# Where the later rows stand beside the first half's layers, and which engine makes a row's gate and diagonals

## The reference, cut to what matters

```
expert, gate = top 16 of 256 candidate pairs, for each of 8 heads      # 128 experts for a token
h   = gelu(einsum('thkd,td->thk', expert_u[expert], x))
out = einsum('thk,thkd->td', gate * h, expert_v[expert])
```

```
s = q k^T * scale, causal;  p = softmax(s);  a = p0 - lam * p1   (layer 1),   a = p   (layer 2)
h = h + (a v) @ w_o
h = h + square(relu(rms_norm(h) @ w_up)) @ w_down
```

## Time and profile before

| | us |
|---|---|
| median of 3 runs | 3049.65 (3047.44 to 3058.9) |
| the profiled execution | 3047.7, its span 3045.9 |
| half 0 from its first product to the end of its second MLP | 1302 to 2315 |
| half 1 | 2327 to 3046 |

### The profile page before, as it was taken

How to read it: one execution, slowest core, us unless ns; L and a number is a source line. 1 busy time by engine, 2 the same in 40 slices (tenths; PEclk the granted TensorE clock), 3 DMA queues, 4 the chain that set the end, 5 groups by cost and what they waited for, 6 DMA issues and landing times. The chain is left out here.

```text
span 3045.9 us, 49365 instructions
## 1 busy us (share of the span) xinstructions
PE 2585.2 (85%) x18974; PEld 1960.1 (64%) x18974; DVE 1763.8 (58%) x3863; ACT 1388.3 (46%) x3129; POOL 1648.2 (54%) x973
## 2 busy tenths in 40 slices
PE   6997977987877777687698997679997999999998
PEld 3865965743333232265477776458776979989998
DVE  5686433767777776765654457565446463256323
ACT  2231222243344343456865456765554454444543
POOL 3822113834444443466287776358883618852785
PEclk8988978999999999888799998889997999999999
DMA  7210013289999999779789997989995415542453
GB/s 293 101 59 26 4 57 152 93 331 421 421 421 421 421 421 415 316 300 401 284 325 401 377 389 296 376 314 393 402 409 218 152 34 175 187 134 74 157 186 115
DMA packets 140538, 797.61 MB, mean 262 GB/s; under 512 B 15504, under 2 KB 18704, under 8 KB 67600
## 3 DMA queue, kind: packets, MB, share of 16 engines
q0 software_dynamic: 73728, 536.90, 43.4%
q1 hardware_dynamic: 65856, 253.09, 23.3%
q10 hardware_dynamic: 720, 4.46, 0.3%
HBM read 787.84 MB, written 6.55 MB: 261 GB/s over the span
## 5 line engine op out<-in xcount | busy, mean ns | idle before, releaser
L303 POOL TENSOR_TENSOR wls<-raws,whs 128x1024 fp32r<-128x1024 f32 (+1 forms) x256 | 612.0, 2400 | 370.3 <-ACT whs L297 368.3
L1998 PE MATMUL ps<-ts,whs 128*128 128x256 f32 x1424 | 292.2, 306 | 27.5 <-DVE ts L2093 19.6
L1754 POOL DMA_INDIRECT raw<-in_peer_uv,un x205 | 209.3, 1021 | 191.7 <-PE ps L1778 87.6
L297 ACT CAST whs<-raws 128x1024 fp32r<-128x1024 f32 (+1 forms) x256 | 263.9, 1036 | 96.8 <-PE ps L2576 35.2
L303 POOL TENSOR_TENSOR wlw<-raws,whw 128x1024 fp32r<-128x1024 f32 x112 | 267.8, 2404 | 70.4 <-ACT whw L297 69.7
L1847 ACT ACTIVATE un<-un 128x1 f32<-128x1 f32 x384 | 77.6, 202 | 445.6 <-DVE scratch L1892 432.0
L1998 PEld LDWEIGHTS ps<-ts,whs 128*128 128x128 f32 x1424 | 239.6, 205 | 56.1 <-issue 26.8
L1892 DVE SCALAR_TENSOR_TENSOR scratch<-raw,ps 128x1024 f32<-128x1024 f32 x149 | 181.4, 1217 | 133.4 <-DMA raw<-in_peer_uv,un 120.2
L2576 PE MATMUL ps<-ts,whs 128*128 128x256 f32 x1216 | 228.7, 289 | 0.2 <-DVE ts L2629 0.2
L1998 PE MATMUL ps<-ts,wls 128*128 128x256 f32 x712 | 209.8, 295 | 0.0
L303 POOL TENSOR_TENSOR wl<-raw,wh 128x2048 fp32r<-128x2048 f32 x23 | 107.1, 4660 | 186.0 <-ACT wh L297 186.0
(11 more groups left out here) (443 smaller groups left out, 6883.2 us busy)
## 6 DMA issues: line engine op xcount, KB each, us to landing
raws<-in_w_up SPq DMA_DIRECT2D x128, 512.0 KB, 4.2
raws<-in_w_down SPq DMA_DIRECT2D x128, 512.0 KB, 4.7
scratch<-in_ada_w SPq DMA_DIRECT2D x17, 1024.0 KB, 13.2
raws<-in_w_qk SPq DMA_DIRECT2D x32, 512.0 KB, 8.5
raw<-in_w_in SPq DMA_DIRECT2D x11, 1024.0 KB, 5.3
raw<-in_peer_w_q SPq DMA_DIRECT2D x8, 1024.0 KB, 8.0
raws<-in_w_v SPq DMA_DIRECT2D x16, 512.0 KB, 5.7
raws<-in_w_o_a SPq DMA_DIRECT2D x16, 512.0 KB, 4.0
```

Of the source, the lines that this page charges most:

```text
L297: e.copy(self.wh[h][:, 0:width], self.raw[slot][:, 0:width]).then_inc(*self.tick("hi", key))
L303: e.tensor_tensor(self.wl[h][:, 0:width], self.raw[slot][:, 0:width], self.wh[h][:, 0:width].bitcast(F32), ALU.subtract).then_inc(*self.ti ...
L1754: e.indirect_dma_start(self.rows[r], None, self.d["peer_uv"], index).then_inc(*self.tick(f"row{r}", n, 16))
L1998: ins = e.matmul(o[:, 0:256], l, r, start=k == 0 and i == 0, stop=k == nk - 1 and i == 2)
```

## The change

- `RATE` falls from 1.1 to 1.0.
- The turns of `attention` weigh 0.01 when n is even and 3.6 when n is odd, instead of 1.2 each.
- For the stacked rows ScalarE only applies Gelu. VectorE multiplies `each32` (32 columns of constants) by Gelu's result and by the gate in one `tensor_scalar` with two column operands (`dve_diagonal`). It stands in VectorE's queue in step n behind the dot of row n+1, and TensorE waits for it in step n+1. The first 256 rows are as before.

The counters give, for half 0 (rows by stage, the same on every engine):

| stage | before | after |
|---|---|---|
| join, q, k, v of layer 1 | 29 | 27 |
| attention of layer 1 | 25 | 32 |
| the norm behind it, w_o | 11 | 10 |
| MLP 1 | 71 | 64 |
| projections of layer 2 | 17 | 16 |
| attention of layer 2 | 25 | 32 |
| w_o of layer 2 | 9 | 8 |
| MLP 2 | 70 | 64 |
| final norm of half 0 | 0 | 4 |

```diff
-RATE = 1.1
+RATE = 1.0
...
-                e.wait_ge(*self.at(A_, ("diag", n)))
+                e.wait_ge(*self.at(D_ if self.stacked(n) else A_, ("diag", n)))
...
         e.wait_ge(*self.at("peer_dve", ("dot", n)))
+        if self.stacked(n):
+            e.activation(gelus[:, c], dots[:, c], ACT.Gelu, bias=0.0, scale=1.0).then_inc(*self.tick(S, ("gelu", n)))
+            return
...
-        if self.stacked(n):
-            e.activation(diag[:, 0:32], self.each32, ACT.Identity, bias=0.0,
-                         scale=weight[:, c]).then_inc(*self.tick(S, ("diag", n)))
...
             if n + 1 < 512:
                 self.dve_dot(e, n + 1)
+            if 0 <= n < 512 and self.stacked(n):
+                self.dve_diagonal(e, n)
...
+    def dve_diagonal(self, e, n):
+
+        k = n % 128
+        e.wait_ge(*self.at("peer_act", ("gelu", n)))
+        e.wait_ge(*self.at("peer_pe", ("acc", n - 4)))
+        e.tensor_scalar(self.diag[1][n % 4][:, 0:32], self.each32, self.gelus[1][:, k:k + 1], self.gate[n // 128][:, k:k + 1],
+                        ALU.mult, ALU.mult).then_inc(*self.tick("peer_dve", ("diag", n)))
...
-            yield 1.2
+            yield 3.6 if n % 2 else 0.01
```

More of the change, by code:

```diff
@@ L1853, in act_weight @@
         e.wait_ge(*self.at(S, ("weight", n)))
-        diag = self.diag[n >= 128][n % 4]
-        if self.stacked(n):
-            e.activation(diag[:, 0:32], self.each32, ACT.Identity, bias=0.0,
-                         scale=weight[:, c]).then_inc(*self.tick(S, ("diag", n)))
-        else:
-            e.activation(diag, self.C("ident"), ACT.Identity, bias=0.0,
-                         scale=weight[:, c]).then_inc(*self.tick(S, ("diag", n)))
+        e.activation(self.diag[n >= 128][n % 4], self.C("ident"), ACT.Identity, bias=0.0,
+                     scale=weight[:, c]).then_inc(*self.tick(S, ("diag", n)))
     def act_join(self, e, tt):
```

## The result

The changed kernel takes 3082.3 us (median of six runs, 3075.7 to 3090.5), the kernel before 3051.3 (six runs, 3044.9 to 3058.9). The ratio is 1.0107, with a 95% interval of 1.0087 to 1.0126: slower by 31 us. The forecast was 3033 in a range of 3008 to 3058, so it had the wrong sign and the time lies outside the range.

A forecast was written before the change was run, and what follows sets the result against it. DMA was taken to bound the MLPs, ScalarE's table loads the first attention's middle. MLPs -33, attentions 0, late diagonals +10, other stages +3, end +5 gave -15, with a more even period -17: 3033 us, range 3008 to 3058.

The forecast's parts named there:

- The MLPs, -33: Both MLPs: transfers set their time, so 64 rows each instead of 71 and 70 save 33 us together.
- The price of a held diagonal: VectorE's diagonal in the MLPs: 0.15 us itself, plus a mean 0.64 us a row waiting for GpSimd's subtractions.
- Rival D: Diagonals make VectorE the MLPs' bound, each waiting 2.1 us: +38, 3088 us, chance 0.13.
- TensorE one row of lag and late diagonals: MLPs: TensorE falls back 2.9 us once and follows late diagonals by up to 2.1 us: +10 together (0 to +20).
- Attentions, 0: Both attentions: seven more rows each cost nothing; between -4 each at the high clock and +7 each at the low.
- the forecast's five terms: Attention's pair of turns: Gelu and table load 1.57, exponentials 0.81, scores 2.13 or 1.30, maximum to dot 2.13, dots 4.50 us.
- Other stages, +3: Projections, w_o stages and norms: fewer rows -3, diagonals on VectorE's path +6, together +3 (-5 to +15).
- The end of half 0, +5: Behind the second MLP and final norm: four rows' steps now come there and delay the join, +5 (0 to +8).

The follow-up runs named there:

- the half gathers: Kernel before, with the gathers of the 256 later rows bringing 1024 of 2048 columns, half the bytes: 3001.9 us, ratio 0.9829.
- the half matmuls: Kernel before, with four of each later row's eight matmuls left out, except the first and last row of every 32: 3050.9 us, ratio 0.9989.
- the odd form: Changed kernel, its diagonal tensor_scalar writing 33 columns and reading its table as 3 times 11 with a gap: 3036.4 us; on the old schedule 3048.5 us.
- The idle operation: Kernel before, diagonals on ScalarE, with VectorE also making gate times diagonal behind each dot into columns nobody reads: 3081.6 us, ratio 1.0097.
- the schedule alone: Kernel before with only the change's rate 1.0 and turn weights 3.6 or 0.01, gate and diagonal staying on ScalarE: 3042.1 us, ratio 0.9973.

## Why the prediction was wrong

- **The MLPs, -33.** The mechanism (transfers set the MLPs) is confirmed by the half gathers and the half matmuls. The size depends on what stands beside it. Moving the rows gave -15 with ScalarE's diagonals, grouped, -23 with the same rows spread evenly, and -29 from the odd form on the old schedule (265.3 and 262.2) to the odd form on the new one (245.9 and 253.0). In the changed kernel it was +7, as held diagonals ate it: 269.0 and 274.6, 45 us more for the pair than in the odd form.
- **The price of a held diagonal is the step that failed.** I took 0.15 us plus a mean wait of 0.64, together 0.79; the means are 0.85 and 0.88 in the two MLPs. The sum is near, by some luck: the 0.15 I took for a quarter of the columns is never under 0.288. What was wrong is what I did with it. I gave 5 us per MLP for the path, with 2.1 us as the longest delay, and laid the rest beside VectorE's slack. But most of the holding comes in holds of 5 us, one diagonal in ten, because GpSimd's subtractions stand two and two without a gap; the earlier trace rows had three in a row in 7.40 us, and I read it as 2.4 us each. All six of the first MLP are on the path, 30 us, and against the odd form the MLPs are 23 and 22 us longer where I had 5 each.
- **Rival D had the right engine and almost the right time (3088) by a sum that did not occur.** It wanted every diagonal to be late by 2.1 us. Its sign, "the dots no longer wait for the DMA", came true: 2.8 us in place of 92.
- **"TensorE one row of lag and late diagonals", +10,** looked for the cost at TensorE. The idle operation, which TensorE doesn't wait for, costs 30 us as well, so VectorE's own lateness is enough for a loss of this size. It was run with the old schedule only, where it falls on other stages; that the changed kernel's MLPs pay for VectorE's lateness and not for TensorE's waits (20 us in each) is argued from it, not shown.
- **Attentions, 0.** The second is at 0 (96.1 for 96.1), the first at +19.5. A pair of turns was to last 10.3 to 11.1 us. From one load of Gelu's table to the next it was 11.67 us with four rows and 10.35 with three in the second attention; in the first it was 13.68 and 11.46, and 16.6 in the first two pairs. In the pair from 1477.00 to 1490.68 three of the forecast's five terms came true at the low clock (0.63 granted there): 0.81, 2.13 and 2.13. The two others failed. The dots took 5.27 for 4.50, four in the place of 3.57 and 1.35 us apart for 1.26, as a diagonal stands between them. And from the last dot's end to the exponential it was 3.34 us for 1.57, because the chain had left out a wait: ScalarE's exponential table is loaded only when the maximum of the even turn's scores (L2492) is there, and TensorE makes these scores (L2318) behind a row's accumulation, which had waited for its diagonal.

```profile
1481.19 1.08 PE L1778 MATMUL ps<-un 128*32 128x256 f32 x8 [0.34 <-DVE un L1884]
...
1482.20 0.80 PE L2318 MATMUL ps<-k,q 64*128 64x128 f32 x4
...
1484.32 1.28 ACT L2399 ACT_TABLE_LOAD   x1 [1.81 <-DVE kept L2492]
```

  This wait stands ahead of seven table loads of the first attention, 12.4 us in all; with the schedule alone it is 2.9, in the kernel before none. The schedule alone makes +13 in the first attention, and the same rows spread evenly +10, so the larger part is the rows' number. Why the kernels divide 211 to 220 us so differently between the two attentions stays open, and so do the two pairs of 16.6.
- **Other stages, +3,** was +14 (layer 1's projections and w_o, layer 2's projections and w_o), and the holds cover it: with the odd form these stages are 16 us shorter than in the changed kernel. **The end of half 0, +5,** measured +3.
- **The size of the schedule's own gain** was overrated in the sum: -33 in the MLPs was not set against what the rows cost in the attentions. Its real balance is -7 to -8 us with ScalarE's diagonals, -12 with free ones and 0 with held ones.

## What to carry to other kernels

Before small work is moved to VectorE, look at what GpSimd runs beside it and for how long without a gap. Here the longest such stretch was a better guide to the price than its share of the time, and what stands behind on VectorE pays it. An operand in PSUM, or a shape that can't be read in two halves, kept a VectorE operation free of it here, for 10 ns at most. Where the time of a stage is set by buffers that go round (gather, dot, diagonal, accumulation), a step made later by one turn lengthens the trip (246 to 281 us and 253 to 288 here). And the even spread with the diagonals left on ScalarE (3034.9 us) was as good as the best kernel with the right values.

## What the runs showed of the hardware

- VectorE's 0.3 us operation on SBUF alone was held for up to 5.15 us beside two GpSimd subtractions of 2.4 us, and was not let in between them. All six long ones of the first MLP start within GpSimd's gather instruction, 0.3 to 0.5 us ahead of the first subtraction's record (1640.94 and 1641.38), so the hold may begin with the gather; the sixteen others of the two MLPs that started within a gather took 0.3 us, and this was not settled.
- The dots show the same, in the kernel before (1223 and 3361 ns at most) as in the changed one. The two rows below are the changed kernel's, with the rows' activations in PSUM (half 0) and in SBUF (ahead of it). Two of the second kind took 3.35 us, both beside two of GpSimd's longer subtractions (9.23 us together).

```profile
L1900 DVE SCALAR_TENSOR_TENSOR scratch<-raw,ps x149: 1203/1211/1222, 1283.8 to 2359.7; 128x1024 f32<-128x1024 f32 x149
...
L1900 DVE SCALAR_TENSOR_TENSOR scratch<-raw,scratch x108: 1200/1224/3358, 610.8 to 1275.2; 128x1024 f32<-128x1024 f32 x108
```

- A quarter of the columns is not a quarter of the time: the 128x32 `tensor_scalar` with two column operands takes 288 ns at best, the 128x128 one with a single one 273.
- TensorE's busy time barely moved when some 260 of its 2147 matmuls in the stretch were left out (252.3 to 251.5 us).
